# Selection rounds in other slots, four banks for turned blocks, and X's first tile as the first transfer, in a two-layer attention and mixture-of-experts kernel

## The reference

```python
def reference(x, ...):
    for l in range(DEPTH):                                   # DEPTH = 2
        h = rms_norm(x, norm_mix_g[l])
        x = x + hybrid_mixer(h, rel_bias, w_in[l], ...)
        h = rms_norm(x, norm_ffn_g[l])
        x = x + hier_moe(h, ...)

def hybrid_mixer(h, ...):
    proj = h @ w_in                                          # 12 parts, 3108 columns
    oa = diff_attention(...)                                 # 4 heads, two softmaxes each, bias by distance
    ob = sliding_sink_attention(...)                         # 8 heads, band of 3 chunks of 64
    oc = dsa_attention(...)                                  # 8 heads on the 128 keys of highest index score
    y = einsum('bsnw,nwd->bsnd', stack([oa, ob, oc]), w_branch)
    gates = sigmoid(h @ w_gate + b_gate)
    return sum(gates * y, axis=2) @ w_out
```

## Time and profile before

| | us |
|---|---|
| median of three runs | 1446.29 |
| lowest, highest | 1444.58, 1446.43 |
| profiled execution | 1445.74 |
| its span in the trace | 1444.0 |

### The profile page before, as it was taken

The page is one execution under the profiler, slowest core; times in us unless marked ns, Lnnn a source line. Parts: engine busy times, 40 slices in busy tenths (PEclk is TensorE's granted clock), DMA queues, the critical chain, the costliest instruction groups (busy, mean ns, idle before and its releaser), DMA issues.

```text
span 1444.0 us, 19326 instructions
## 1 busy us (share of the span) xinstructions
PE 1389.4 (96%) x6778; PEld 1017.8 (70%) x6778; DVE 751.1 (52%) x1907; ACT 499.1 (35%) x1186; POOL 762.7 (53%) x643
## 2 busy tenths in 40 slices
PE   6999999999999999999689999999999999999997
PEld 5778867777777866556377887777777778566553
DVE  4487865656674146222146687755567543452221
ACT  4322333343432133334243333333443412234331
POOL 4556654444445524676555565454544554266763
PEclk9999999999999999999989999999999999999999
DMA  6334322223212848999732232222222147589995
GB/s 202 119 113 147 89 78 71 70 79 100 86 60 73 285 163 287 318 351 338 208 119 76 59 116 88 78 59 85 78 86 87 59 142 268 190 274 330 328 345 137
DMA packets 148563, 225.30 MB, mean 156 GB/s; under 512 B 18480, under 2 KB 95722, under 8 KB 148458
## 3 DMA queue, kind: packets, MB, share of 16 engines
q1 hardware_dynamic: 136264, 198.58, 42.6%
q0 software_dynamic: 9648, 16.81, 4.9%
q10 hardware_dynamic: 2546, 8.57, 1.5%
HBM read 216.51 MB, written 31.25 MB: 172 GB/s over the span
## 4 chain that ended last, share of the span: by engine, by line
PE 88%; DVE 5%; ACT 2%; issue 1%; POOL 1%; DMA 1%; SPq 1%; POOLq 0%; DVEq 0%
PE bank L820 19%; PE bank L822 18%; PE bank L821 18%; PE bank L1080 16%; PE bank L987 4%; PE bank L999 3%; PE bank L1020 2%; PE bank L1066 2%; PE bank L1010 1%; PE bank L940 1%; DVE probs L1748 1%; POOL w_lo L710 1%; PE bank L953 1%; PE bank L874 1%; DMA probs<-normed_dram,slot_token 1%
## 5 line engine op out<-in xcount | busy, mean ns | idle before, releaser
L706 POOL TENSOR_SCALAR w_hi<-raw 128x1024 fp32r<-128x1024 f32 (+2 forms) x144 | 150.3, 1044 | 437.5 <-PE bank L822 433.8
L710 POOL TENSOR_TENSOR w_lo<-raw,w_hi 128x512 fp32r<-128x512 f32 (+2 forms) x288 | 360.4, 1273 | 12.0
L821 PE MATMUL bank<-w_hi,hT_lo 128*128 128x512 f32 (+2 forms) x696 | 259.3, 372 | 0.0
L1080 PE MATMUL bank<-work,ptmp 128*128 128x512 f32 x512 | 228.7, 600 | 2.7 <-ACT ptmp L1431 2.7
L820 PE MATMUL bank<-w_lo,hT_hi 128*128 128x512 f32 (+2 forms) x576 | 217.2, 377 | 2.8 <-POOL w_lo L710 1.4
L822 PE MATMUL bank<-w_hi,hT_hi 128*128 128x512 f32 (+2 forms) x576 | 212.2, 368 | 0.0
L1080 PEld LDWEIGHTS bank<-work,ptmp 128*128 128x128 f32 x512 | 96.0, 193 | 112.8 <-issue 109.3
L772 POOL TENSOR_TENSOR w_lo<-work,w_hi 128x512 fp32r<-128x512 f32 x120 | 148.3, 1262 | 43.0 <-ACT w_hi L1441 42.9
L820 PE MATMUL bank<-hT_lo,w_hi 128*128 128x512 f32 x384 | 159.7, 416 | 0.0
L822 PE MATMUL bank<-hT_hi,w_hi 128*128 128x512 f32 x384 | 150.8, 393 | 0.0
L821 PE MATMUL bank<-hT_hi,w_lo 128*128 128x512 f32 x384 | 150.5, 392 | 0.0
(11 more groups left out here) (293 smaller groups left out, 2340.3 us busy)
## 6 DMA issues: line engine op xcount, KB each, us to landing
work<-in_w_ff_gate SPq DMA_DIRECT2D x66, 512.0 KB, 9.1
work<-in_w_ff_up SPq DMA_DIRECT2D x66, 512.0 KB, 10.6
work<-in_w_ff_down SPq DMA_DIRECT2D x33, 1024.0 KB, 6.4
raw<-in_w_gate SPq DMA_DIRECT2D x48, 512.0 KB, 3.9
raw<-in_w_in SPq DMA_DIRECT2D x40, 512.0 KB, 3.6
raw<-in_w_branch SPq DMA_DIRECT2D x24, 512.0 KB, 3.6
raw<-in_w_out SPq DMA_DIRECT2D x16, 512.0 KB, 3.7
normed_dram<-mixed ACTq DMA_DIRECT2D x8, 512.0 KB, 2.6
```

Of the source, the lines that this page charges most:

```text
L706: nc.gpsimd.tensor_scalar(w_hi[:, two, :, 0:w], raw[:, slot, :, 0:w], 1.0, 0.0, ALU.mult, ALU.add).then_inc(split_hi, 1)
L710: last = nc.gpsimd.tensor_tensor(w_lo[:, two, kk, 0:w], raw[:, slot, kk, 0:w], w_hi[:, two, kk, 0:w].bitcast(F32), ALU.subtract)
L821: nc.tensor.matmul(out_ap, s_lo, m_hi, start=False, stop=False)
L1080: last = nc.tensor.matmul(G[e % 2][:, :], et[:, e % 2, kt * P:(kt + 1) * P], work[:, n % RING, kk, :], start=(kt == 0), stop=(kt == KT - 1))
```

## The change

Three things. The six late rounds go to slots 1, 2, 3, 5, 9 and 13. Each block of a chunk is turned into a bank of its own, `T[0]`, `T[1]`, `S[0]`, `S[1]`; block 0 waits for all copies of earlier chunks, block 2 for the last index ReLU. X's first tile and the gain row are issued ahead of the tables, the first weight unit ahead of X's last tile; SyncE writes the bias table to DRAM, behind the parameters, instead of ScalarE, and ScalarE copies that table after X's first sum of squares and takes the fourth sum of squares after the first `norm_hi` in both layers. Beside these the reciprocals of `job_inv` are kept for eight jobs instead of four.

```diff
+ROUND_SLOTS = (1, 2, 3, 5, 9, 13)
...
-        job_inv = sb("job_inv", [P, 4, 2])
+        job_inv = sb("job_inv", [P, 8, 2])
...
+        turn_banks = (T[0], T[1], S[0], S[1])
...
-            sp.dma_start(probs[0:N_BUCKETS, 1, 0:REL_HEADS], rel_bias).then_inc(pre_b, 16)
-            sp.dma_start(aqT[0:N_BUCKETS, 0:2, 0:SPAN // 2],
-                         bucket_onehot.rearrange("b (a n) -> b a n", a=2)).then_inc(pre_b, 16)
-            sp.dma_start(ident[:, :], identity).then_inc(pre_i, 16)
...
             sp.dma_start(X[:, 0, :], x[0, 0:P, :]).then_inc(x_in[0], 16)
             gain_rows(0)
+            sp.dma_start(probs[0:N_BUCKETS, 1, 0:REL_HEADS], rel_bias).then_inc(pre_b, 16)
+            sp.dma_start(aqT[0:N_BUCKETS, 0:2, 0:SPAN // 2],
+                         bucket_onehot.rearrange("b (a n) -> b a n", a=2)).then_inc(pre_b, 16)
+            sp.dma_start(ident[:, :], identity).then_inc(pre_i, 16)
             for t in range(1, TT):
+                if t == TT - 1:
+                    first_units(0, [0])
                 sp.dma_start(X[:, t, :], x[0, t * P:(t + 1) * P, :]).then_inc(x_in[t], 16)
-            first_units(0)
+            first_units(0, range(1, RAW_SLOTS))
             parameters(0)
+            sp.wait_ge(pre_row, 2)
+            sp.dma_start(toep.rearrange("h (a n) -> h a n", a=2),
+                         akT[0:REL_HEADS, 0:2, 0:SPAN // 2]).then_inc(pre_toep, 16)
             constants()
...
                     n = fills[0]
-                    if n >= 2:
-                        pe.wait_ge(t_free, n - 1)
+                    if b == 0 and n:
+                        pe.wait_ge(t_free, n)
+                    if b == 2 and c:
+                        pe.wait_ge(relu_done, IDX_HEADS * (TT - 1))
                     for t in range(TT):
-                        last = nc.tensor.transpose(T[n % 2][:, t * P:(t + 1) * P],
+                        last = nc.tensor.transpose(turn_banks[b][:, t * P:(t + 1) * P],
                                                    chunk_rows[c % 2][:, t, b * P:(b + 1) * P], ident[:, :])
...
-                    src = T[n % 2][:, :]
+                    src = turn_banks[b][:, :]
...
-            for a in range(2):
-                act.wait_ge(pre_mm, a + 1)
-                nc.scalar.activation(akT[0:REL_HEADS, a, 0:SPAN // 2], G[a][0:REL_HEADS, 0:SPAN // 2],
-                                     ACT.Copy, scale=-1.0).then_inc(pre_row, 1)
-            act.wait_ge(pre_row, 2)
-            act.dma_start(toep.rearrange("h (a n) -> h a n", a=2),
-                          akT[0:REL_HEADS, 0:2, 0:SPAN // 2]).then_inc(pre_toep, 16)
+            def table_rows():
+                for a in range(2):
+                    act.wait_ge(pre_mm, a + 1)
+                    nc.scalar.activation(akT[0:REL_HEADS, a, 0:SPAN // 2], G[a][0:REL_HEADS, 0:SPAN // 2],
+                                         ACT.Copy, scale=-1.0).then_inc(pre_row, 1)
...
                 for t in range(3):
                     norm_squares(t)
-                if l == 0:
-                    norm_squares(3)
+                    if l == 0 and t == 0:
+                        table_rows()
                 norm_hi(0)
-                if l:
-                    norm_squares(3)
+                norm_squares(3)
...
-                    if 1 <= s <= len(rounds) - rounds_done:
-                        top_round(*rounds[rounds_done + s - 1])
+                    if s in ROUND_SLOTS:
+                        top_round(*rounds[rounds_done + ROUND_SLOTS.index(s)])
```

More of the change, by code:

```diff
@@ L525, in constants, with first_units @@
                     sp.dma_start(dst, src).then_inc(pre_c, 16)
-            def first_units(l):
-                for unit in range(RAW_SLOTS):
+            def first_units(l, which=range(RAW_SLOTS)):
+                for unit in which:
                     w = P_CHUNKS[units[unit][1]][2]
@@ L1739, in post @@
                 v.wait_ge(exp_done, g + 1)
-                link(nc.vector.reciprocal(job_inv[:, st, :], job_sum[:, st, :]))
+                link(nc.vector.reciprocal(job_inv[:, g % 8, :], job_sum[:, st, :]))
                 if job.name == "A":
-                    link(nc.vector.tensor_scalar(job_mix[:, st:st + 1], job_sum[:, st, 0:1], job_inv[:, st, 1:2],
+                    link(nc.vector.tensor_scalar(job_mix[:, st:st + 1], job_sum[:, st, 0:1], job_inv[:, g % 8, 1:2],
                                                  neg_lam[:, 0:1], ALU.mult, ALU.mult))
@@ L1747, in post @@
                     for m in range(2):
-                        last = nc.vector.tensor_scalar(p[:, m, 0:nk], p[:, m, 0:nk], job_inv[:, st, m:m + 1], None,
+                        last = nc.vector.tensor_scalar(p[:, m, 0:nk], p[:, m, 0:nk], job_inv[:, g % 8, m:m + 1], None,
                                                        ALU.mult)
@@ L1757, in rows_out @@
                     v.wait_ge(t_done, rows_fill[b - 2] + 1)
-                nc.vector.tensor_scalar(o_rows[:, b % 2, i, :], O[:, i * P:(i + 1) * P], job_inv[:, g % 4, 0:1], None,
+                nc.vector.tensor_scalar(o_rows[:, b % 2, i, :], O[:, i * P:(i + 1) * P], job_inv[:, g % 8, 0:1], None,
                                         ALU.mult).then_inc(o_free, 1)
```

## The result

| | before, us | after, us |
|---|---|---|
| median | 1446.15 | 1428.66 (1427.69 to 1431.6, 4 runs) |
| profiled execution | 1445.74 | 1428.42 |
| its span | 1444.0 | 1426.6 |

Both medians were measured side by side. By the medians 17.5 us are won, 4.7 us more than forecast, and the time lies 1.8 us under the low end of the range.

What follows compares the result with a forecast made beforehand. TensorE was taken as the bound, 88% of the span on the chain that ended last. Banks 5.2, late rounds 5.4, clock 1.5 and start 0.7 sum to 12.8 us: 1446.29 to 1433.5 us, range 1430.5 to 1440, chance 0.58.

Steps and rivals of the forecast that it cites:

- the low end of the range: Largest gain, 15.9 us, 1430.4, including 1.5 if the clock is kept once more elsewhere; the range given starts at 1430.5.
- banks: Turns of projection chunks: TensorE no longer waits for ScalarE to empty a bank, 5.2 us (bounds 3.4 and 7.1).
- late rounds: Slot 8: without slot 6's round VectorE's line 1744 ends before GpSimd's split; TensorE's stall goes, 2.7 us a layer, 5.4.
- start: First 25 us: VectorE's 0.90 us wait for ScalarE's copy of the turned first tile closes, 0.7 us (-1.5 to +1.9).
- clock behind slot 8, layer 1: Job 6 to job 8 takes 8.03 us against layer 0's 6.50; without the stall the clock stays full, 1.5 us.
- clock at the first experts: First expert in both layers: the forecast had no term for a lower clock there, 0 us.
- the pitch: Turn of a chunk: 0.126 us per weight load, so sixteen make 2.02 us and the turn loses 0.55.
- Rival C: Turns: the waits are worth only what the matmul view shows, 3.4 instead of 5.2 us: 1435.3; chance 0.08.
- Rival A: Slot 8: line 1744 meets GpSimd's split again, 0.75 us a layer left, clock still falls once: 1436.5; chance 0.15.
- Rivals B and E: B: start loses, -1.5 instead of +0.7, 1435.7, chance 0.12; E: late table write delays staircase copies and weight loads, slower, 0.03.

Runs made afterwards that it cites:

- the filler: 20 (layer 0) and 24 (layer 1) filler matmuls instead of 16 before the first expert's wait: before 1441.65, after 1429.48; before with moved rounds 1435.67, with banks 1434.58.
- the two runs of the start: Kernel before with the whole new start (transfer order, table write on SyncE, ScalarE's order): 1445.36; with only ScalarE's later fourth sum of squares in layer 0: 1446.23.
- The kernel with six fillers: Kernel after with 6 instead of 16 filler matmuls ahead of TensorE's wait for the first expert's gathered rows: 1434.08 (0.9921).

## Why the prediction fell short

**The account.** Set side by side, in us:

| term | forecast | measured | from |
|---|---|---|---|
| banks | 5.2 | 6.7 | steps in the traces; 6.7 alone, 6.3 to 7.1 with the filler |
| late rounds | 5.4 | 5.3 | 2 x 2.63 in the traces; 5.2 to 6.0 with the filler |
| start | 0.7 | about 0.4 | see below |
| clock behind slot 8, layer 1 | 1.5 | 1.5 | 4.15 - 2.63 |
| clock at the first experts | 0 | 3.3 | 2 x 1.7, less what is left of it in after |
| sum | 12.8 | 17.2 | measured 17.5 |

With the filler in both, and so at nearly equal clock, before and after are 1441.65 and 1429.48: 12.2 us, where the forecast without its clock term was 11.3. The mechanisms of the change were sized nearly right. Two things were not.

**The banks, mis-sized by 1.5 us.** The step was the pitch: "eight loads without a wait take 1.02 us ... 0.126 us apiece". Sixteen loads in one go take 1.87 us to the load behind, not 2.02. The single starts show why. In this turn the second load, where each of these views begins, comes 0.23 us after the first (81.04 before, 79.61 after), and from there on the loads follow each other every 0.109 us in both kernels, except where before waits. Weight loads, before and then after:

```profile
81.27 0.47 PEld L940 LDWEIGHTS bank<-ident,mixed 128*128 128x128 f32 x4
```

```profile
79.84 0.36 PEld L948 LDWEIGHTS bank<-ident,mixed 128*128 128x128 f32 x3
```

So the 0.126 was the pitch with a start of 0.12 us spread over eight loads, and the forecast charged that start twice. The start is paid once, whatever the length of the run: 0.23 + 15 x 0.109 = 1.87. The turn loses 0.70 and not 0.55 us, which over eight turns and two of chunk I (0.57 instead of 0.45) is the 1.5. Rival C, only what the matmul view shows (3.4), is refuted: the loads' waits of 7.1 us were the better bound.

**The clock, missing by 3.3 us.** The step was to look for lower clock only behind the stall that the change removes. The low end allowed "another 1.5 if the clock is kept once more elsewhere" as a scrap; it was kept twice. A look at the granted clock in all stretches of before would have shown three low ones besides the layer boundary and the last 4 us, at 532, 928 and 1245, each with slow matmuls behind a wait. The row of before's first expert (8.79 us for 16 matmuls whose like takes 7.10) stood in the trace and I did not compare it. What I could not have read there is that the change would help at two of them, since it does nothing to those waits. Even now this is only partly explained. Shown: the lower clock there costs 1.7 us a layer (8.79 against 7.10), filling the wait takes it away in before (five executions of five, by the mean clock), a longer wait brings it into after (both layers of the trace, and six executions of six by the mean clock), and it comes and goes between executions of one kernel. The kernel before has executions of its own at 1442.2 us with a mean clock of 0.993 and others at 1447.4 with 0.989. Open: why at an equal wait before falls in most executions and the kernels with moved rounds in few. With the rounds alone the clock was 0.992 to 0.994, with the banks alone 0.988 to 0.992, so it goes with the rounds; whether with the vanished stall itself or with the distances in time between waits was not tried. The mean clock is a coarse sign of this: the traces of after and of after with the filler have no fall at any of these places and still 0.992 and 0.994, by the length of the low stretch at the layer boundary. That the filler at the experts also cleared the clock in slot 8, far from it, hints at the distances, but nothing here shows it. The stall of 2.35 us in layer 1's slot 8 was followed by the lower clock in the four traces with 16 fillers (before, the banks, the two runs of the start), all of which had it at the first expert before, and in neither of the two with more.

The Trainium skill, page "TensorE: Matmul & The Clock Gate", section "HAM oscillation", says that a long enough wait between groups of matmuls lowers the clock, and that it is paid at each such wait. The kernel with six fillers agrees (3.29 and 4.37 us, slow in every execution by the mean clock). For the shorter waits of this case "each time" does not hold: of the twelve stalls of 2.35 us in the six traces that still have them, five were followed by the lower clock (four in layer 1, one in layer 0) and seven were not.

**The late rounds, right.** Line 1750 is short, ends 0.13 us before the split begins and 0.26 before TensorE's load; the stall is gone whole. The 2.7 a layer is 2.63. Rival A did not come: it needed the split beside line 1750. Before, line 1744 and `scale_rows` behind it (line 1772) lay beside the split's subtractions (line 710). GpSimd, then VectorE, in the kernel before:

```profile
214.34 2.81 POOL L710 TENSOR_TENSOR w_lo<-raw,w_hi 128x512 fp32r<-128x512 f32 x2
```

```profile
215.95 1.75 DVE L1772 TENSOR_TENSOR o_rows<-o_rows,o_rs 128x512 f32<-128x512 f32 x1
```

In the kernel after, line 1750 is over before the split and takes 0.62 instead of 1.67. `scale_rows` starts 0.22 us ahead of the split, overlaps its first 0.46 us and takes 0.68 instead of 1.75; there it is the split's first instruction that is longer, 1.37 instead of 1.05 us. The Trainium skill, page "SBUF — State Buffer", section "Who interferes with whom", gives as the reason that a VectorE instruction with two inputs in SBUF contends with a GpSimd instruction that reads SBUF. These durations agree with it.

**The start, right in sign and not provable in size.** Rows of the kernel after: TensorE's table matmuls, ScalarE's copies and second sum, VectorE's subtractions, SyncE's write of the table:

```profile
6.77 2.32 PE L833 MATMUL bank<-work,probs 32*20 32x320 f32 x4 [6.77 <-DMA work<-in_bucket_onehot]
```

```profile
9.12 0.43 ACT L1465 ACTIVATE work<-bank 20x320 f32<-20x320 f32 x1 [0.64 <-PE bank L833]
9.46 1.04 ACT L1269 ACTIVATE ptmp<-X 128x1024 f32<-128x1024 f32 x1
```

```profile
12.83 1.28 DVE L1581 TENSOR_TENSOR hT_lo<-bank,hT_hi 128x512 fp32r<-128x512 f32 x2
...
21.08 1.29 DVE L1581 TENSOR_TENSOR hT_lo<-bank,hT_hi 128x512 fp32r<-128x512 f32 x2 [0.57 <-ACT hT_hi L1278]
```

```profile
13.58 0.94 SPq L606 DMA_DIRECT2D toeplitz_dram<-work  x1
```

The tables' data came at 6.77 (estimated 7.3), the copies ended at 9.55 (10.2), the second sum began 0.56 earlier than before, VectorE's wait of 0.90 for the first copy is gone, and its last subtraction is 0.86 earlier. Rivals B and E did not come: the table is issued at 13.58 and the first staircase copy at 17.29. But 0.86 is one execution. Where GpSimd splits the third unit, the five other traces with the new start or ScalarE's new order stand -0.07 to 0.59 us ahead of before, and the six without either -0.36 to 0.49. The means are about 0.4 and 0.1. It is small, and the start varies by as much from execution to execution.

## What to carry to other kernels

List the granted clock of all short stretches first and compare equal groups of matmuls with each other; a group that takes 8.8 us where its like takes 7.1 is a cost of the wait ahead of it, and such costs move when anything earlier is moved. To price a part of a change, measure it also on a kernel whose clock-prone waits are filled: the rounds looked worth 9.6 us and were worth 5 to 6. And take the pitch of a pipelined instruction from the starts of single instructions, and what a run of them costs at its beginning apart from it.

## What the runs showed of the hardware

- Waits of TensorE of 1.0 and 0.8 us (2.0 and 0.8 in layer 1) with eight transposes between them had the lower clock behind them in 8 of 8 cases in the traces of kernels with the late rounds as before, and in 2 of 8 with these rounds moved; 3.3 and 4.4 us brought it in both layers of the trace and, by the mean clock, in all six executions.
- One such fall costs 1.5 to 1.7 us, and 2.5 to 2.9 where it begins with the turns ahead of the matmuls (0.63 + 2.28, 0.88 + 1.65, 0.88 + 1.90).
- The weight loads of 128 x 128 float32 transposes in a row start every 0.109 us, at full clock; between the first two of a turn lie 0.23 us in some turns and 0.06 in others.
- A 128 x 384 VectorE instruction with two inputs in SBUF took 1.67 us beside a GpSimd split and 0.62 alone; begun ahead of the split, a 128 x 512 one kept its 0.68 us and the split's first instruction took 1.37 instead of 1.05.
- With four filler matmuls more at layer 0's first expert, slot 8 of layer 1, 395 us later, kept the full clock in the trace behind the same 2.35 us wait, and the mean clock of 0.993 to 0.994 says the same of the other four executions. With the banks as well, the trace again shows both stalls of 2.35 us at full clock, but two of six executions were 2 us slower at 0.992. Why is open.
